# Layer norm of a two-layer backbone: the squares of the next chunk moved directly behind the root, and the new stream values made by GpSimd instead of ScalarE and VectorE

## What is computed

```
def layer_norm(x, g, b):
    xc = x - jnp.mean(x, -1, keepdims=True)
    return xc * lax.rsqrt(jnp.mean(xc * xc, -1, keepdims=True) + NORM_EPS) * g + b

x_lat = layer_norm(DN_ALPHA * x_lat + m_lat[2] * y_lat, ln_g[l, 0], ln_b[l, 0])
f_lat = swiglu(modulate(x_lat, m_lat[3], m_lat[4]), w_ffn_in[l], w_ffn_out[l])   # x * (1 + scale) + shift
x_lat = layer_norm(DN_ALPHA * x_lat + m_lat[5] * f_lat, ln_g[l, 1], ln_b[l, 1])
```

## Time and profile before

| | |
|---|---|
| median of 3 runs | 4148.32 us (4141.9 to 4148.87) |
| profiled execution, its own time | 4146.43 us |
| span of its trace | 4145.0 us |
| PE busy | 3721.5 us (90%) |
| DVE busy | 1767.1 us (43%) |
| ACT busy | 1066.2 us (26%) |
| POOL busy | 208.4 us (5%) |

### The profile page before, as it was taken

How to read it: one execution, slowest core, us unless ns; L and a number is a source line. 1 busy time by engine, 2 the same in 40 slices (tenths; PEclk the granted TensorE clock), 3 DMA queues, 4 the chain that set the end, 5 groups by cost and what they waited for, 6 DMA issues and landing times. The chain is left out here.

```text
span 4145.0 us, 52262 instructions
## 1 busy us (share of the span) xinstructions
PE 3721.5 (90%) x22354; PEld 2997.6 (72%) x22354; DVE 1767.1 (43%) x1933; ACT 1066.2 (26%) x1473; POOL 208.4 (5%) x118
## 2 busy tenths in 40 slices
PE   7998568979889999999998999468978989999997
PEld 5887446458767888888886888336467768888886
DVE  3112857656343332332325212757656343333334
ACT  2000422456233111111114100422455141111113
POOL 0000003012000000000000000002021000000000
PEclk9999769989999999999999999679989989999998
DMA  8433540031421111111103632340042211111211
GB/s 247 107 86 113 187 154 19 13 103 44 161 92 46 31 31 45 46 30 30 46 20 122 147 91 102 130 152 11 11 123 84 85 46 46 46 46 46 61 35 41
DMA packets 294824, 318.74 MB, mean 77 GB/s; under 512 B 42398, under 2 KB 261130, under 8 KB 294410
## 3 DMA queue, kind: packets, MB, share of 16 engines
q1 hardware_dynamic: 269034, 267.43, 21.6%
q0 software_dynamic: 6912, 30.15, 2.4%
q10 hardware_dynamic: 18720, 18.88, 1.4%
HBM read 247.78 MB, written 71.59 MB: 77 GB/s over the span
## 5 line engine op out<-in xcount | busy, mean ns | idle before, releaser
L566 PE MATMUL psum<-h_hi,lead_hi 128*128 128x512 f32 (+1 forms) x1432 | 392.4, 369 | 14.8 <-DVE h_lo L1090 8.7
L566 PE MATMUL psum<-h_lo,lead_hi 128*128 128x512 f32 (+1 forms) x1432 | 390.4, 368 | 0.0
L566 PE MATMUL psum<-h_hi,lead_lo 128*128 128x512 f32 (+1 forms) x1432 | 390.1, 368 | 0.0
L1213 DVE SCALAR_TENSOR_TENSOR y<-psum,mods,y 128x1024 f32<-128x1024 f32 (+1 forms) x264 | 260.4, 1014 | 259.9 <-PE psum L566 259.0
L566 PEld LDWEIGHTS psum<-h_hi,lead_hi 128*128 128x128 f32 x1432 | 251.5, 190 | 63.2 <-DVE h_lo L1090 9.7
L1178 ACT CAST f_whi<-lead_raw 128x1024 fp32r<-128x1024 f32 x44 | 46.3, 1053 | 945.1 <-PE psum L566 934.5
L566 PEld LDWEIGHTS psum<-h_hi,lead_lo 128*128 128x128 f32 x1432 | 251.1, 190 | 45.9
L566 PEld LDWEIGHTS psum<-h_lo,lead_hi 128*128 128x128 f32 x1432 | 251.2, 190 | 45.7
L566 PE MATMUL psum<-h_hi,w_hi 128*128 128x512 f32 (+1 forms) x856 | 229.0, 369 | 37.6 <-DVE w_lo L827 26.5
L1226 DVE TENSOR_TENSOR f_hid<-f_silu,psum 128x1280 f32<-128x1280 f32 (+1 forms) x44 | 59.6, 1354 | 460.8 <-PE psum L566 336.2
L716 DVE COPY lin_stage<-psum 128x1280 f32<-128x1280 f32 (+1 forms) x48 | 68.9, 1435 | 438.3 <-PE psum L566 438.3
(11 more groups left out here) (280 smaller groups left out, 6187.1 us busy)
## 6 DMA issues: line engine op xcount, KB each, us to landing
lead_raw<-in_w_ffn_in SPq DMA_DIRECT2D x88, 512.0 KB, 6.2
ada_w<-in_w_ada SPq DMA_DIRECT2D x30, 1024.0 KB, 11.3
lead_raw<-in_w_in SPq DMA_DIRECT2D x48, 512.0 KB, 5.3
proj_cm<-lin_stage POOLq DMA_DIRECT2D x38, 640.0 KB, 4.2
f_raw<-in_w_ffn_out SPq DMA_DIRECT2D x44, 512.0 KB, 3.8
ada_w<-in_w_ada ACTq DMA_DIRECT2D x18, 1024.0 KB, 5.6
na_qk<-proj_cm SPq DMA_DIRECT2D x48, 320.0 KB, 7.6
hg_pj<-proj_cm SPq DMA_DIRECT2D x20, 640.0 KB, 9.3
```

What stands on the lines that cost most here:

```text
L566: ins = nc.tensor.matmul(out[:, t0:t0 + tn], w, h[:, t0:t0 + tn], start=start and n == 0, stop=stop and n == 2)
L1213: ins = nc.vector.scalar_tensor_tensor(out=y[:, o, t0:t1], in0=sets(o + 1)[:, t0:t1], scalar=gate[:, o, m:m + 1], in1=y[:, o, t0:t1], op0= ...
```

## The change

In `residual_norm` two things are edited. First, `square(i+1)` on ACT moves from behind `modulated(i-1)` and `mod_copy(2i)` to directly behind `root(i)`; this holds for all four stages. Second, in stages 1 to 3 the new stream values are no longer made by ACT and DVE: GpSimd gets a stream of its own, which for each chunk waits for `modulated(c)` and then makes all eight blocks with eight `tensor_scalar` instructions of 128x256 (times g, plus b, both read per partition from `vecs`). The two semaphores of the halves become one, and in stage 2 SP waits for it ahead of the store. Nothing else is edited; the lines behind the edit have other numbers.

```
@@ residual_norm, sync
                 for c in range(n_c):
                     if store:
-                        sp.wait_ge(s_xa.h, s_xa.at(c + 1))
-                        sp.wait_ge(s_xd.h, s_xd.at(c + 1))
+                        sp.wait_ge(s_xp.h, s_xp.at(c + 1))
                         sp.dma_start(chunk(k.x_dram, c), chunk(y, c)).then_inc(s_out.h, 16)
...
+            @block.gpsimd
+            def _(pool):
+                for c in range(0 if last else n_c):
+                    pool.wait_ge(s_h.h, s_h.at(c + 1))
+                    for j in range(KB):
+                        x = y[:, j, c * T:(c + 1) * T]
+                        ins = nc.gpsimd.tensor_scalar(x, x, g_ln[:, j:j + 1], b_ln[:, j:j + 1], ALU.mult, ALU.add)
+                    ins.then_inc(s_xp.h, 1)
...
@@ scalar
                     if i < n_c:
                         root(i)
+                    if i + 1 < n_c:
+                        square(i + 1)
                     if 1 <= i <= n_c and last:
                         act.wait_ge(s_u.h, s_u.at(i))
                         new_x(i - 1, KB, s_x)
...
                     if i < n_c:
                         mod_copy(2 * i)
-                    if i + 1 < n_c:
-                        square(i + 1)
                     if i >= 1 and not last:
                         upper(i - 1)
-                        new_x(i - 1, XA, s_xa)
                     if i < n_c:
                         mod_copy(2 * i + 1)
@@ vector
-                def new_x(c):
-                    dve.wait_ge(s_h.h, s_h.at(c + 1))
-                    for j in range(XA, KB):
-                        x = y[:, j, c * T:(c + 1) * T]
-                        ins = nc.vector.tensor_scalar(x, x, g_ln[:, j:j + 1], b_ln[:, j:j + 1], ALU.mult, ALU.add)
-                    ins.then_inc(s_xd.h, 1)
...
                     if i >= 1 and not last:
-                        new_x(i - 1)
                         lower(i - 1)
```

More of the change, by code:

```diff
@@ L879, in residual_norm @@
     n_c = tokens // T
-    XA = KB // 2
     store = sub == 1 and not last
@@ L905, in residual_norm @@
         else:
-            s_h, s_hi, s_lo, s_xa, s_xd = (sem(x) for x in ("ln_modulated", "ln_hi", "ln_lo", "ln_new_x_act", "ln_new_x_dve"))
+            s_h, s_hi, s_lo, s_xp = (sem(x) for x in ("ln_modulated", "ln_hi", "ln_lo", "ln_new_x"))
         s_out = sem("x_stored") if store else None
@@ L1122, in residual_norm @@
     else:
-        for x in (s_h, s_hi, s_lo, s_xa, s_xd):
+        for x in (s_h, s_hi, s_lo, s_xp):
             x.done(n_c)
```

## The result

The changed kernel takes 4110.59 us, the median of 4 runs (4110.15 to 4114.82), against 4145.11 of before beside it (4 runs, 4138.2 to 4148.87). The ratio is 0.9921, 95% interval 0.9906 to 0.9935, so some 34 us faster. The forecast was 4162 us, 13 slower; its range began at 4126.

What follows compares the result with a forecast made beforehand. In the norm stages no engine is full, so a chain through several sets the pace. Stages 1 to 4 at +6.4, +6.3, +9.5 and -9 sum to +13 on 4148.3, giving 4162 us; range 4126 to 4200.

Steps and rivals of the forecast that it cites:

- the one who has the access keeps it over a queue without gaps: SBUF access in stages 1 to 3: GpSimd's eight instructions hold off `lower`, which starts 6.0 instead of 2.1 us behind modulated values.
- Whether GpSimd and DVE block each other: Step on SBUF access shared by GpSimd and DVE: they do block each other, and this decides the sign of the change.
- The two waits for GpSimd's eight: Loop and tail of stages 1 to 3: each wait lasts eight GpSimd instructions, 6.0 us, making the loop 16.5 us.
- the lower bound of 0.66: Cost of one GpSimd instruction of 256 columns: at least 0.66 us, from the two-input form's 2.37 us for 1024 columns.
- the forecast's own slope: Stages 1 to 3: 9.6 us for each 0.1 us of GpSimd instruction, from four waits of eight instructions in three stages.
- access passes after each instruction: Rival for stages 1 to 3: `lower` waits 0.4 us on average; sum -19, 4129 us; chance 0.30 with fast instructions.
- GpSimd work free and unblocked: Rival for stages 1 to 3: loop 12.6 us, tails 2.1 us shorter; 4114 us, chance 0.05.
- the new loop: Norm stages: squares 1.91, modulated 4.03, copy and `upper` 2.13, `lower` 2.29, `centre` 2.28; 12.6 us without contention.
- The 16 us: Stage 1, root(2) to root(3): the forecast's middle step in 10.2+16+16.5 = 42.7 us from root(1) to root(4).
- in the steady part the moved squares are worth little: Steady part of the stages: the new loop of 12.6 us is only 0.9 us below the old pace.
- the contention put on top: Stages 1 to 3: GpSimd's queue of eight delays `lower`, taking the loop from 12.6 to 16.5 us and lengthening the tails.

Runs made afterwards that it cites:

- the trial with a queue of two-input sums: Changed kernel plus, at the start of stage 4, four GpSimd two-input sums of 256 columns queued against three VectorE products; read from its trace: they alternate one for one.
- the version with `centre` first: Changed kernel with `centre(i+2)` on DVE directly behind `unit(i)`, ahead of `lower(i-1)`; 4091.87 us, ratio 0.9869 to the kernel before.
- order only: Kernel before with only the squares moved directly behind the root, new stream values still on ACT and DVE; 4112.18 us, ratio 0.9920.
- GpSimd only: Changed kernel with the squares put back behind the modulated values, so only GpSimd's work is new; 4137.10 us, ratio 0.9984 to the kernel before.

## Why the prediction was wrong

**The step that failed** is "the one who has the access keeps it over a queue without gaps", as applied to GpSimd's eight in "Whether GpSimd and DVE block each other". It was read from the earlier trace rows, in which VectorE is the one that keeps it. That half is right: it kept GpSimd out for 4.69 us over two instructions. The other half, GpSimd keeping VectorE out, had only single instructions behind it, and the trial with a queue of two-input sums shows it passing after each, one for one. So `lower` began 2.0 us behind the modulated values and not 6.0, and the loop is 12.48 us, where 12.6 stood for it without contention and 16.5 with it. The two waits for GpSimd's eight that the sum has in the loop, and the two in the tail, are not there: root(1) to root(4) of stage 1 took 34.7 us against 42.7 forecast, its tail 20.8 against 29.7, stage 3's last step 13.2 against 16.3 and its tail 19.2 against 31.

**A term that was mis-sized:** GpSimd's instruction, 0.75 us from the earlier trace rows, is 0.54, below the lower bound of 0.66. The row was of one operation, and two are cheaper (0.91 against 0.55 us with scalars per partition). By the forecast's own slope, 9.6 us for each 0.1, this error alone would have brought +13 to -7.

**The rival that came true** is "access passes after each instruction", at -19 us. With 0.54 in place of 0.75 and its slope of 7 us for each 0.1 it gives -19 - 15 = -34. Measured were -34.5 by the medians and -32.6 in the stages. The bounds did not include 0.54, so the range ended at 4126, above the result. That the -34 meet is in part luck. This rival had GpSimd end last in the tails; at 0.54 its last instruction ends ahead of PE's in all three (1265.10 for 1267.89, 2268.88 for 2271.62, 3336.46 for 3336.63). Only the store behind it still ends stage 2, 22.9 us behind the last root, for 28.2 in the rival.

**A rival that fits as well by its number** is "GpSimd work free and unblocked", with a chance of 0.05: it had 4114 us and -10.5, -8.5, -6 and -9 for the stages, where -8.9, -8.9, -5.5 and -9.3 were measured. The time cannot part the two. The traces do: GpSimd's fifth instruction took 2.59 us under `lower`, and the trial in which sums and products alternate shows VectorE blocked too. In the loop this blocking is nearly free, as `lower` is 0.05 us late, and so the free rival's sum comes close.

**What was right:** root(1) came 4.3 us sooner behind root(0) in stage 1, where 4.2 stood; stage 4 is 51.1 us long, where 51.4 stood; stage 3's step from root(1) to root(2) is 8.04 us for 8.2; the new loop, its members and its length without contention; that it bounds the steady part, which the version with `centre` first confirmed.

**A small term that was mis-sized:** root(1) to root(2) was put at 10.2 us and took 9.36. The sum has 1.4 us for each of two modulation products, which take 1.07 in its own rows. The 16 us that it has for root(2) to root(3) stands there without its working; 11.57 were measured.

**How the halves weigh:** "in the steady part the moved squares are worth little" holds for root(2) to root(4), two steps a stage: 24.9 us with order only, 27.0 before. The two steps before are bound by PE, at 9.56 and 9.36 us, where 13.85 and 13.63 stood, and there is the gain of stages 1 and 2; the prediction's sum had these two steps (-4.2, and 10.2 for 13.5), and it was the contention put on top that turned the sign. Order only is worth 31 us in the stages, while taking new values off ScalarE and VectorE is worth 1.8, which becomes 12 only when `centre` no longer waits.

## What to carry to other kernels

When two engines block each other, ask which of them the row shows winning: a queue that starves its rival in one direction says nothing on the other. Take the cost of an instruction from a row of the same form or bound it in both directions, and do not assume that more operations cost more. When two mechanisms give the same time, as here the free and the passing one, let the traces decide and not the total. After a reorder, look at which wait now ends last in each step: here a second move on the other engine, of one instruction past another, brought more than half as much again as the whole change.

## What the runs showed of the hardware

- GpSimd's tensor_scalar of 256 float columns: 0.83 us with one operation and a constant, 0.91 with one and a scalar per partition, 0.39 with two and constants, 0.55 with two and scalars per partition. At 1024 columns, 2.77 and 1.07 us for one and for two operations with constants, and 1.19 for two with scalars.
- The access to SBUF is uneven. GpSimd is shut out over a whole queue of long VectorE instructions with two SBUF inputs (4.69 us over two) and slowed to 1.2 to 1.5 us an instruction over short ones of 0.33; in these traces VectorE waits at most for the one GpSimd instruction that is under way (2.01 us instead of 0.41 beside a sum of 1024 columns), and its long products and `lower` are at most 0.2 us late behind GpSimd's short one-input ones in the changed kernel, 0.4 in the kernel with GpSimd only.
- VectorE's instruction with one input from PSUM did not slow GpSimd: 0.54 us apart beside `centre`.
- TensorE's variance of sixteen matmuls took 3.72 us at the full granted clock, without a wait ahead of it, and 5.41 us at a mean of 0.68 behind 2.5 us of waiting for the squares.
